# Pairs of heads in block and sliding attention: scores side by side in both row halves, the sink as a score column, the mask pass yielding the bias

## The reference

```python
# block attention: 8 heads of 64, slope_h = 2 ** -(h + 1)
s = q @ k.T * 64 ** -0.5 - slope_h * (tq - tk)      # where tk <= tq, else -1e30
out = softmax(s) @ v

# sliding attention: 16 query heads, 4 key heads, |i - j| <= 128, a sink logit per head
s = where(abs(i - j) <= 128, q @ k.T * 64 ** -0.5, -inf)
m = max(max(s), sink);  e = exp(s - m)
out = (e / (sum(e) + exp(sink - m))) @ v
```

## Time and profile before

| what | value |
|---|---|
| median of 3 runs | 2156.73 us (2155.37 to 2157.11) |
| the profiled execution | 2155.41 us, its span 2153.6 us |
| PE busy | 2037.9 us, 95% of the span |
| DVE busy | 1248.1 us, 58% |
| POOL busy | 1051.1 us, 49% |
| ACT busy | 898.6 us, 42% |
| mean granted TensorE clock | 0.976 of full speed |
| chain that ended last | PE 79%, DVE 14%, ACT 3%, issue 2% |

### The profile page before, as it was taken

The page is one execution under the profiler, slowest core; times in us unless marked ns, Lnnn a source line. Parts: engine busy times, 40 slices in busy tenths (PEclk is TensorE's granted clock), DMA queues, the critical chain, the costliest instruction groups (busy, mean ns, idle before and its releaser), DMA issues.

```text
span 2153.6 us, 25797 instructions
## 1 busy us (share of the span) xinstructions
PE 2037.9 (95%) x9428; PEld 1655.5 (77%) x9428; DVE 1248.1 (58%) x2233; ACT 898.6 (42%) x1745; POOL 1051.1 (49%) x779
## 2 busy tenths in 40 slices
PE   7999997999999789999999999988999999999986
PEld 5777886788888667777888888876677888888875
DVE  6564215243332768986774556556797474664655
ACT  4444233433333435444444333434565444433342
POOL 5324445444444545552666565535432466656541
PEclk9999998999999889999999999999999999999998
DMA  4112231233223111111222332312000223223221
GB/s 153 58 50 79 98 98 59 82 109 103 88 92 107 59 50 58 52 51 58 98 98 98 100 100 86 107 59 92 30 30 30 98 95 102 92 85 112 93 80 49
DMA packets 48510, 174.24 MB, mean 81 GB/s; under 512 B 5376, under 2 KB 5632, under 8 KB 48384
## 3 DMA queue, kind: packets, MB, share of 16 engines
q1 hardware_dynamic: 48384, 172.60, 24.0%
HBM read 170.48 MB, written 2.10 MB: 80 GB/s over the span
## 4 chain that ended last, share of the span: by engine, by line
PE 79%; DVE 14%; ACT 3%; issue 2%; POOL 1%; DMA 1%; SPq 0%; DVEq 0%; POOLq 0%; ACTq 0%
PE b L382 23%; PE b L384 23%; PE b L383 23%; PE b L404 2%; PE b L396 2%; DVE ssq L474 1%; DVE ra L468 1%; PE b L416 1%; PE b L417 1%; PE b L434 1%; PE b L415 1%; DVE h L664 1%; PE b L397 1%; PE b L398 1%; DVE ra L586 1%
## 5 line engine op out<-in xcount | busy, mean ns | idle before, releaser
L232 POOL TENSOR_TENSOR ra<-raw,ra 128x512 fp32r<-128x512 f32 x632 | 857.7, 1374 | 916.8 <-ACT ra L268 916.1
L382 PE MATMUL b<-ra 128*128 128x512 f32 x2528 | 1010.9, 400 | 51.1 <-DVE ra L468 29.3
L384 PE MATMUL b<-ra 128*128 128x512 f32 x2528 | 993.0, 393 | 0.0
L383 PE MATMUL b<-ra 128*128 128x512 f32 x2528 | 992.8, 393 | 0.0
L382 PEld LDWEIGHTS b<-ra 128*128 128x128 f32 x2528 | 480.3, 190 | 156.2 <-issue 32.6
L384 PEld LDWEIGHTS b<-ra 128*128 128x128 f32 x2528 | 479.7, 190 | 102.9
L383 PEld LDWEIGHTS b<-ra 128*128 128x128 f32 x2528 | 480.6, 190 | 93.8
L268 ACT ACTIVATE ra<-raw 128x512 fp32r<-128x512 f32 x632 | 380.5, 623 | 317.5 <-PE b L384 266.3
L593 DVE TENSOR_TENSOR tmp<-b,rb 128x512 f32<-128x512 f32 x78 | 53.3, 690 | 179.9 <-PE b L384 179.9
L678 DVE TENSOR_TENSOR fa<-b,fa 128x512 f32<-128x512 f32 x136 | 90.4, 686 | 79.9 <-PE b L384 79.4
L273 ACT ACTIVATE ra<-tmp 128x512 fp32r<-128x512 f32 x89 | 55.8, 630 | 160.6 <-DVE tmp L733 81.8
(11 more groups left out here) (240 smaller groups left out, 2023.0 us busy)
## 6 DMA issues: line engine op xcount, KB each, us to landing
raw<-in_f_g SPq DMA_DIRECT2D x40, 512.0 KB, 3.5
raw<-in_f_v SPq DMA_DIRECT2D x40, 512.0 KB, 3.5
raw<-in_f_d SPq DMA_DIRECT2D x40, 512.0 KB, 3.5
raw<-in_w_up SPq DMA_DIRECT2D x32, 512.0 KB, 3.5
raw<-in_w_down SPq DMA_DIRECT2D x32, 512.0 KB, 3.5
raw<-in_p_g SPq DMA_DIRECT2D x16, 512.0 KB, 3.5
raw<-in_w_gp SPq DMA_DIRECT2D x8, 512.0 KB, 3.4
raw<-in_w_ga SPq DMA_DIRECT2D x8, 512.0 KB, 3.5
```

The costliest lines, as they stand in the source:

```text
L232: e.tensor_tensor(wl, src, wh.bitcast(F), ALU.subtract).then_inc(*w_low.mark(n))
L382: e.matmul(ps, wh[:, c:c + 128], xh, start=start, stop=False)
L383: e.matmul(ps, wh[:, c:c + 128], xl, start=False, stop=False)
L384: last = e.matmul(ps, wl[:, c:c + 128], xh, start=False, stop=stop)
```

## The change

Block and sliding attention get a function of their own, `attention_pairs`. Differential attention keeps `attention`.

- Two heads (2p in rows 0 to 63, 2p+1 in rows 64 to 127) are scored in the same slot, one behind the other, every second slot. So eight slots still hold two heads. Exponentials of both come in the next slot, reciprocals and normalizations in the one after. A head's turns begin 6 slots after the pair's first scores (second head: 10), one in each slot; the value products stand in odd slots.
- The mask pass now computes (scores + mask) times minus the scale and takes the minimum, so that its accumulated value is the bias itself; the exponential takes scale -1.0. The separate `bias` instruction is gone.
- With sinks, the sink is column 384 of the score bank. DVE copies it there for the first tile of each head (`sink_column`), ahead of that head's scores, and the score waits for the copy. The mask tile gets a zero column beside it, so maximum and sum take the sink in. The second exponential (L315) and `add_sink` (L578) are gone. The mask pass and the exponential are one column wider.
- The normalization stays on DVE in block attention and moves to POOL in sliding attention.
- The band mask is loaded in two pieces (one more DMA), with two one-column memsets; the wait of DVE for the mask ahead of the sliding stage is gone, and the mask passes wait for it instead.

```diff
+        elif kind == "normalize" and a[2] == "p":          # gpsimd_program
+            p, su, _, inverse = a
+            w.wait_ge(*inverse)
+            e.tensor_scalar(p, p, su, 1.0, ALU.mult, ALU.mult).then_inc(*els.mark(n))
...
         elif kind == "exp":
-            p, nm, sl, su, es, sink, bias_done = a
-            w.wait_ge(*bias_done)
-            e.activation(p, p, ACT.Exp, bias=nm, scale=sl, accum_out=su).then_inc(*soft.mark((n, 0)))
-            if es is not None:
-                e.activation(es, sink, ACT.Exp, bias=nm).then_inc(*soft.mark((n, 1)))
+            p, nm, su, min_done = a
+            w.wait_ge(*min_done)
+            e.activation(p, p, ACT.Exp, bias=nm, scale=-1.0, accum_out=su).then_inc(*soft.mark(n))
...
-            e.tensor_tensor_reduce(p, banks[b][:, 0:nk], mk, 1.0, -BIG, ALU.add, ALU.max,
-                                   mx).then_inc(*soft.mark(n))
-        elif kind == "bias":
...
-        elif kind == "add_sink":
...
+            e.tensor_tensor_reduce(p, src, mk, -sl, BIG, ALU.add, ALU.min, nm).then_inc(*soft.mark(n))
+        elif kind == "sink_column":
+            b, t, free = a
+            for f in free:
+                w.wait_ge(*f)
+            e.tensor_copy(banks[b][:, 384:385], m.sink8[:, t:t + 1]).then_inc(*soft.mark(n))
...
+        def scores(t, i):
...
+            if before_scores:
+                before_scores(t, i, b)
+            n = row("score", b, c0(i), nk, (qh, ql), (kh, kl), rw, i, lo, bank_free[b], (*qt, *kt_))
+            done("pe", "score", n)
+            mk, made = mask_of(t, i)
...
+            n = row("mask_min", p[:, 0:wide], banks[b][:, c0(i):c0(i) + wide], mk, slope(t), nm, (m.sig("score"), n),
+                    (*free, *made))
+            v = done("ve", "soft_v", n)
+            bank_free[b] = (v,)
...
+        for p in range(npairs):
+            for i in range(4):
+                s0 = 8 * p + 2 * i
+                at(s0, lambda p=p, i=i: both(scores, p, i), 0.6)
+                at(s0 + 1, lambda p=p, i=i: both(expo, p, i), 1)
+                at(s0 + 2, lambda p=p, i=i: both(invert, p, i), 0.55)
+                at(s0 + 2, lambda p=p, i=i: both(normalize, p, i), 0.7)
+            for z in range(2):
+                t, s0 = 2 * p + z, 8 * p + lat + 4 * z
+                for i in range(4):
+                    at(s0 + i, lambda t=t, i=i: turn(t, i), 1)
+                at(s0 + 1 + lat_v, lambda t=t: pv(t, 0), 0)
+                at(s0 + 3 + lat_v, lambda t=t: pv(t, 1), 0)
...
-    att_done = attention("moba", 8, 4, 3, 2, Q1, K1, V1, lambda i: (0, 128 * (i + 1)), O1, ahead,
-                         lambda s: (2 if s < 6 else 3) if s < 24 else 2, PT1)
+    att_done = attention_pairs(4, 6, 2, Q1, K1, V1, lambda i: (0, 128 * (i + 1)), lambda i: 0, None,
+                               lambda t, i: (m.mask[:, 384 - 128 * i:512], ()), lambda t: 2.0 ** -(t + 1), O1, ahead,
+                               lambda s: (2 if s < 6 else 3) if s < 24 else 2, PT1, "v")
...
-    t_m = load(m.mask[:, 0:384], A["band"], *now("ve"))
-    row("hold", "dve", (t_m,))
+    masked = now("ve")
+    t_band = (load(m.mask[:, 0:384], A["band"], *masked), load(m.mask[:, 385:641], A["band"][:, 0:256], *masked))
+    n = row("zero_columns", masked)
+    t_band += (done("ve", "soft_v", n),)
+    sunk = {}
+
+    def before_scores(t, i, b):
+        if i == 0:
+            sunk[t] = (done("ve", "soft_v", row("sink_column", b, t, bank_free[b])),)
+            bank_free[b] = sunk[t]
...
+    attention_pairs(8, 6, 2,
...
+                    before_scores, mask_of, lambda t: 0.125, O1, ahead, lambda s: 1 if s < 64 else 2, PT3, "p")
```

More of the change, by code:

```diff
@@ L390, in tensor_program @@
         elif kind == "score":
-            b, nk, (qh, ql), (kh, kl), row, i, lo, free, ready = a
+            b, c0, nk, (qh, ql), (kh, kl), row, i, lo, free, ready = a
             for t in free + ready:
                 w.wait_ge(*t)
-            ps = m.banks[b][:, 0:nk]
+            ps = m.banks[b][:, c0:c0 + nk]
             rr, qs, ks = slice(row, row + 64), slice(128 * i, 128 * i + 128), slice(lo, lo + nk)
@@ L563, in vector_program @@
                                    op1=ALU.add).then_inc(*soft.mark(n))
-        elif kind == "mask_max":
-            p, b, nk, mk, mx, score_done, free = a
+        elif kind == "mask_min":
+            p, src, mk, sl, nm, score_done, free = a
             w.wait_ge(*score_done)
@@ L976, in build @@
         h_tok += [(load(h[:, a:b, :], A["x"][:, a:b, :]),)] * (b - a)
-    t_cst = load(m.mask[:, :], A["alibi"])
+    t_cst = load(m.mask[:, 0:S], A["alibi"])
     n = row("constants")
@@ L1086, in s_tile @@
             assert rw == krow
-            n = row("score", b, hi - lo, (qh, ql), (kh, kl), rw, i, lo, bank_free[b], (*qt, *kt_))
+            n = row("score", b, 0, hi - lo, (qh, ql), (kh, kl), rw, i, lo, bank_free[b], (*qt, *kt_))
             bank_free[b] = None
@@ L1094, in soft @@
             d = {}
[L1095 to L1140, removed]
+            base = 24 + 8 * (k % 4)
@@ L1142, in bias @@
+            a = P[t % 2][i]
+            ti, pb, tfree = T.get()
+            mx, nm, su = (sm[:, base + 2 * z:base + 2 * z + 2] for z in range(3))
+            parts = []
+            for comp in range(2):
+                b, nk, ts = s_tile(t, i, comp)
+                n = row("row_max", mx[:, comp:comp + 1], b, ts, free2)
+                v = done("ve", "soft_v", n)
+                parts.append((b, (a, pb)[comp], (p_free.get(k, ()), tfree)[comp]))
             def bias():
-                d["m"] = done("ve", "soft_v", row("bias", nm, mx, s8, sl, v))
+                d["m"] = done("ve", "soft_v", row("bias_diff", nm, mx, v))
@@ L1145, in expo @@
             def expo():
[L1146 to L1149, removed]
-                    n = row("exp", a, nm, sl, su, es, vc("sinks", t), d["m"])
-                    d["x"] = done("ac", "soft_a", (n, 1))
+                n = row("exp_diff", parts, nm, su, d["m"])
+                d["x"] = done("ac", "soft_a", (n, 1))
+                for c, (b, _, _) in enumerate(parts):
+                    bank_free[b] = ((m.sig("soft_a"), (n, c)),)
```

131 lines of the change are left out of this document (108 added, 23 removed).

## The result

The changed kernel takes 2161.71 us at the median of 19 runs (2157.92 to 2163.93), the kernel before 2155.37 in the runs beside it (2153.59 to 2157.24). The ratio is 1.0028, 95% interval 1.0021 to 1.0034: slower by 6.3 us. The profiled executions have spans of 2160.4 and 2153.6 us, 6.8 apart, so they can be compared row by row.

The account below looks back on a forecast made before the run. PE was taken to bound both stages, DVE nearly a second bound in sliding attention. Terms: -12.0 + 1 - 28.2 + 28.0 + 0.8 + 14 + 1 = +4.6 us on 2155.4; forecast 2161 us, range 2141 to 2174.

Parts of the forecast that it names:

- The sink copy's stall: Sliding attention, first scores of a pair: wait for a copy in DVE's queue, 4.0 us each, seven times, 28.0 us.
- PE's own work: Sliding attention: two heads take 15.04 us of PE against 18.56, so -28.2 us over eight pairs.
- The scores' overlap: Both stages: the second head's score products cost PE nothing beside the first's where both banks are free.
- The clock: Sliding attention: falls behind most stalls, 2.0 us each, 14 for seven; 1 more for later turns at the stage's end.
- Block attention: Whole stage: 12.0 us saved, 1 added for turns and value products three slots later at its end; -11 us.
- the waits of a pair's scores are on banks read two slots before: Block attention: a pair's scores wait only on such banks, with 2 or 3 linear steps between; no cost taken.
- merged scores: Block attention: 32 score trios become 16, with less cost of entering a score; 12.0 us saved.
- POOL's normalization: Sliding attention: 64 normalizations on POOL, 0.64 and 0.96 us for 256 and 384 columns; no cost taken.
- the clock holds: Rival, sliding attention: falls in only two of seven stalls, or DVE somewhat ahead with shorter stalls; 2147 us, chance 0.27.
- The copy is free: Rival, sliding attention: DVE so far ahead that the copy is done when PE comes; 2125 us, chance 0.07.

Follow-up runs that it names:

- early_copy: Changed kernel with the sink copies issued two slots earlier, behind the last mask passes of the pair before: 2128.01 us, ratio 0.9872 to the kernel before.
- same_rows: early_copy with the second head of each pair reading the first head's row half of queries and keys: 2144.64 us, ratio 0.995 to the kernel before.
- block_only: Changed kernel with pairs in block attention alone, sliding attention as in the kernel before: 2150.06 us, ratio 0.9971 to the kernel before.
- v_turn: early_copy with the value tile's turn one linear step later in block attention's first 24 slots: 2125.23 us, ratio 0.9861 to the kernel before.
- low_first: Changed kernel with low parts of block attention's turns issued to DVE at the start of the next slot: 2161.09 us, ratio 1.0022 to the kernel before.
- out_first: early_copy with only the output's low part in sliding attention issued at the next slot's start, ahead of the rope: 2128.8 us, ratio 0.9877 to the kernel before.
- both_copies: Changed kernel with both heads' sink copies issued together ahead of head A's scores, same slot: 2145.22 us, ratio 0.9948 to the kernel before.
- block_pool: early_copy with block attention's normalization given to POOL too: 2132.05 us, ratio 0.9892 to the kernel before.

## Why the prediction was right

The time was 2161 and came out 2161.7. The terms, against the profiled executions:

- **The sink copy's stall, +28.0.** Take a pair with one short fall of the clock, 1584.90 to 1605.62: 20.72 us, less 1.7 of clock, less PE's own 15.04, leaves 3.98. I had 4.0 for each of seven. A is late by 3.0 (predicted 2.8), B by 1.22 (1.2). That is so for five of the seven. Pair two's A waits 0.85 less. Pair eight's copy has no rope in front of it, though I had written one, but low parts that wait for ACT. The seven together come to some 27. Right in the main, and early_copy shows it by taking it away.
- **PE's own work, 15.04 for two heads.** Shown by early_copy: 16.57 less a wait that costs 1.53. The scores' overlap is shown by same_rows.
- **The clock, +14 and +1.** The stage loses 20.5 us to it and lost 8.7 before: +11.8. But the parts differ from mine. The seven new falls lose 18.8 and not 14; I took 2.0 each, and they come in sizes near 1.7 and 3.4. In time, by the distances between scores, they cost some 15.5 (an estimate: 1.55 for each of three, 2.5 to 3.0 for each of four), so the 14 was near. The step that failed is that I took nothing off for falls of the old stage, and added 1 for its end. In the kernel before the clock fell at 1653 to 1665, behind a wait of 0.71, and lost 5.1 us there, and 3.6 at and ahead of the first pair; the changed kernel has its last stall at 1648 and 1.00 from 1656 on, and loses 1.7 at the first pair. That makes 7.0 less. In block_only the old stage loses as much at another place, so what was there to be read is the 8.7 of the stage, not a fall at its end.
- **Block attention, -11; it was -5.7.** The step that failed is "the waits of a pair's scores are on banks read two slots before" with nothing said of turns. Moving turns three slots moved them against the value tile's turn, which takes one of the two turn banks; the turn behind it needs the bank of the turn one slot before, whose low part stands in DVE's queue behind the value tile's. Three waits of 4.93 against one of 1.16 before, 1.7 of clock behind the longest, and 2.66 against 2.14 at the end: -12 + 3.8 + 1.7 + 0.5 = -6.0. The 12.0 of merged scores therefore holds within what these sums can tell; v_turn and low_first show the mechanism of the waits by taking them away, and v_turn that a fall of the clock at the end takes back half of what this gives.
- **POOL's normalization.** I scaled it to 0.64 and 0.96 for 256 and 384 keys; it takes 0.53 on average (33.5 us for 64), and DVE's was 0.508. No cost was right while PE stalled; with early copies it is the next thing late (out_first).

```profile
L259 POOL TENSOR_SCALAR fa<-fa,sm 128x256 f32<-128x256 f32 (+1 forms) x64 | 33.5, 532 | 36.3 <-DVE sm L553 36.2
```

The Trainium skill, page "GPSIMD Engine Reference", 4.1 Engine selection, says that one-input work runs at about DVE's rate there while two-input work is twice as slow. The trace agrees with the second half: 1.27 against 0.68 us for the products of 512 columns at 1562.14 (POOL) and 1561.95 (DVE). With the first it agrees by the means, 532 against 508 ns. But DVE's mean has nine instructions of over 1 us in it, and its median is 410 ns against 533 on POOL; for 256 keys most take 0.34 on DVE, and 0.48 on POOL. So one-input work was 1.3 to 1.4 times slower here, not twice. An estimate from that page would have been 0.5 and not 0.64, with the same sum.

So the sum was right partly because two errors met: block attention 5 us too good, sliding attention 3 us too bad. Of the rivals, "the clock holds" has one run behind it, both_copies, where it held behind three of eight pairs; its 2147 is near the 2145 of that run, by another road. "The copy is free" gave 2125, with 6.4 us in it for B's wait. early_copy makes the copy free for both heads of seven pairs and still reaches only 2128, since block attention gives 5 us less than I had and new waits stand behind the copy's.

**Open.** Why the clock holds behind some stalls of 2.91 us in both_copies and falls behind others was not settled, and each clock loss is that of one profiled execution. No run took away the two waits at the end of block attention, 1.16 and 1.50; block_pool took normalizations from DVE there and met POOL instead. The sink as a column and the mask pass that yields the bias were not tried apart from the rest.

## What to carry to other kernels

A small instruction put at the head of a bounding engine's row costs what stands in front of it in its own queue, not its length: 0.15 us of copy cost PE 3 to 4 us, seven times, and issuing it two slots earlier, once its bank was free, turned +0.3% into -1.3% against the kernel before. When all of one kind of work is moved by some slots, look for what else shares its banks at the new place. And a stall has a second price in the granted clock: add up the clock lost by stage in the kernel before, too, since a change can remove a fall as well as make one, and take the sum of a stage, not the place of one fall.

## What the runs showed of the hardware

- An idle time of 2.91 us was followed by a fall of the clock behind three pairs and by none behind two others (both_copies). With a second wait of 0.60 behind a thin trio a fall followed every time, in all eight pairs of the changed kernel. In the kernel before, a fall followed a wait of 0.71 at 1653.48; in block_only none followed the same wait of 0.70 at 1652.83.
- A fall lost 1.7 us of clock or 3.4. In time the small one cost 1.55 us, from first to second scores of a pair (both_copies), the large one 0.9 to 1.4 more (the changed kernel).
- Six score products of 384 keys in two row halves, one head's three issued ahead of the other's, take 0.72 us (early_copy); in one half 1.25 (same_rows). For 256 keys 0.56 and 0.91.
- A one-column DVE copy from SBUF to PSUM takes 0.154 us (16 of them, 2.5 us), as a one-column reciprocal does (0.158), both in the changed kernel.
- A scaling of 256 columns by one factor per row takes 0.48 us on POOL (the changed kernel) and mostly 0.34 on DVE (the kernel before).
